# The norms of a two-layer decoder: worked tile by tile on ScalarE and VectorE, turned in eight banks, weights applied at the copy

## The reference

```python
def rms_norm(x, w):
    y = x * lax.rsqrt(jnp.mean(x * x, axis=-1, keepdims=True) + 1e-6)
    return y * w

for l in range(2):
    xn = rms_norm(x, norm1_w[l])
    x = x + token_mixer(xn, w_in[l], ...)       # RG-LRU, forgetting attention, mLSTM on columns of xn @ w_in
    x = x + peer_ffn(rms_norm(x, norm2_w[l]), peer_wq[l], ...)   # q = xn @ wq, top-k keys, experts u, v
return rms_norm(x, final_norm_w)
```

## Time and profile before

| | |
|---|---|
| median of 3 runs | 4875.45 us (4859.12 to 4879.31) |
| the profiled execution | 4877.19 us, its span 4875.4 us |
| mean granted TensorE clock | 0.963 |
| PE busy | 4450.7 us (91%) |
| DVE busy | 3228.7 us (66%) |
| ACT busy | 1769.6 us (36%) |
| POOL busy | 2717.0 us (56%) |
| DMA | 892.84 MB, mean 183 GB/s |

### The profile page before, as it was taken

The page is one execution under the profiler, slowest core; times in us unless marked ns, Lnnn a source line. Parts: engine busy times, 40 slices in busy tenths (PEclk is TensorE's granted clock), DMA queues, the critical chain, the costliest instruction groups (busy, mean ns, idle before and its releaser), DMA issues.

```text
span 4875.4 us, 73068 instructions
## 1 busy us (share of the span) xinstructions
PE 4450.7 (91%) x21194; PEld 3685.9 (76%) x21194; DVE 3228.7 (66%) x5017; ACT 1769.6 (36%) x3206; POOL 2717.0 (56%) x1477
## 2 busy tenths in 40 slices
PE   7899999889888998999879999998898898989998
PEld 5766775679888897777757668666798888977776
DVE  5755124448889876888867451243588897768888
ACT  2234123114555652333322441231145556533332
POOL 5743663655456664555458337536555566745553
PEclk9999999999999999999989999999999999999999
DMA  2211221124588999999722112212246789999996
GB/s 107 77 53 35 82 78 44 69 72 137 178 251 260 310 311 322 339 342 335 279 68 86 47 37 86 74 39 82 74 141 193 239 268 295 327 327 336 337 336 250
DMA packets 463087, 892.84 MB, mean 183 GB/s; under 512 B 41376, under 2 KB 320416, under 8 KB 459808
## 3 DMA queue, kind: packets, MB, share of 16 engines
q1 hardware_dynamic: 387424, 617.22, 38.8%
q0 software_dynamic: 73728, 268.47, 15.9%
q10 hardware_dynamic: 1728, 4.89, 0.3%
HBM read 787.65 MB, written 102.76 MB: 183 GB/s over the span
## 4 chain that ended last, share of the span: by engine, by line
PE 56%; DVE 15%; issue 13%; DMA 8%; POOL 3%; ACT 3%; SPq 1%; DVEq 0%; ACTq 0%; POOLq 0%
PE pair L767 7%; DMA ring<-v_tab 6%; PE bank L767 6%; PE bank L1145 5%; PE bank L1150 5%; PE bank L1140 4%; PE bank L793 3%; PE pair L770 3%; PE pair L793 3%; PE bank L770 3%; PE bank L931 2%; PE bank L1088 2%; DVE qk L2128 2%; DVE ring L2095 2%; PE bank L946 1%
## 5 line engine op out<-in xcount | busy, mean ns | idle before, releaser
L649 POOL TENSOR_TENSOR w_hi<-ring,ones 128x1024 fp32r<-128x1024 f32 x272 | 535.8, 1970 | 895.0 <-PE bank L793 272.4
L637 POOL TENSOR_TENSOR w_lo<-ring,w_hi 128x1024 fp32r<-128x1024 f32 x256 | 634.4, 2479 | 556.2 <-ACT w_hi L1473 555.3
L1088 PE MATMUL bank<-xT,w_hi 128*128 128x384 f32 x2048 | 726.3, 355 | 42.5 <-ACT gst L1485 39.1
L1088 PE MATMUL bank<-xl_peer,w_hi 128*128 128x384 f32 x2048 | 703.7, 344 | 0.0
L652 POOL TENSOR_TENSOR w_lo<-ring,w_hi 128x1024 fp32r<-128x1024 f32 x272 | 691.7, 2543 | 21.3
L1479 ACT CAST w_hi<-ring 128x1024 fp32r<-128x1024 f32 x252 | 265.5, 1053 | 675.6 <-PE bank L1150 446.1
L1473 ACT CAST w_hi<-ring 128x1024 fp32r<-128x1024 f32 x256 | 268.8, 1050 | 640.4 <-DVE ring L2095 546.4
L2187 DVE TENSOR_TENSOR cl<-att,ch 128x384 fp32r<-128x384 f32 x256 | 356.5, 1393 | 174.3 <-ACT ch L1544 164.1
L643 POOL TENSOR_TENSOR w_lo<-ring,w_hi 128x1024 fp32r<-128x1024 f32 x126 | 301.9, 2396 | 281.9 <-ACT w_hi L1479 281.9
L1088 PEld LDWEIGHTS bank<-xT,w_hi 128*128 128x128 f32 x2048 | 402.0, 196 | 45.8 <-ACT w_hi L1473 36.6
L1140 PE MATMUL bank<-w_hi,ch 128*128 128x512 f32 x1536 | 394.3, 392 | 22.6 <-ACT ch L1544 22.3
(11 more groups left out here) (324 smaller groups left out, 9315.9 us busy)
## 6 DMA issues: line engine op xcount, KB each, us to landing
ring<-v_tab SPq DMA_DIRECT2D x252, 512.0 KB, 6.6
ring<-w_stream SPq DMA_DIRECT2D x240, 512.0 KB, 3.2
ring<-u_tab SPq DMA_DIRECT2D x512, 128.0 KB
g_spill<-gst SPq DMA_DIRECT2D x256, 192.0 KB, 3.6
hn<-u_tab SPq DMA_DIRECT2D x256, 128.0 KB
x_last<-u_tab SPq DMA_DIRECT2D x256, 128.0 KB
w_spill<-vg SPq DMA_DIRECT2D x12, 2048.0 KB, 9.5
w_spill<-att SPq DMA_DIRECT2D x12, 2048.0 KB, 10.2
```

Of the source, the lines that this page charges most:

```text
L637: nc.gpsimd.tensor_tensor(w_lo[s % 2][:, :], ring[2 + s % 2][:, :], w_hi[s % 2][:, :].bitcast(F32), ALU.subtract)\
L649: nc.gpsimd.tensor_tensor(w_hi[b][:, 0:n], src, ones[:, 0:1].to_broadcast([P, n]), ALU.mult)\
L1088: nc.tensor.matmul(out, w_hi[s % 2][:, c * P:(c + 1) * P], dense_parts(c)[part], start=(c == 0 and part == 0), stop=False)
```

## The change

- The token factors are worked tile by tile. ACT squares (Square with a row sum, halves of 512 columns) and takes the root of one tile's mean while the next tile is squared; DVE makes mean and reciprocal. For N1 the order of tiles is 3, 0, 1, 2; the squares of a tile start when its values are added, and the last value chunk and the last chunk of "OUT" are ordered by tile, with a semaphore for each.
- For N1 x itself is turned, with an ordinary float32 matmul against the identity times the token factors (`diagonal`); for N2 the scaled rows are turned, with an ordinary matmul against the identity. Chunks 0 to 3 of a tile are turned as soon as the tile is there. All eight banks are used.
- The norm's weights are applied when a chunk is copied, from columns `nwc`, which are loaded by five more DMAs of ACT's queue; the row `nwb` is only needed for the gathered tile and is loaded at the layer's start.
- The first product behind a norm waits for high and low chunks one by one (`first_high_low`).
- POOL splits the gate's weights into buffer 1 and the first LRU chunk into buffer 0 before it waits for the gate product.
- `layer_done` is given before DVE adds the banks; the last `add_row` writes x instead of `pair`. ACT waits for x at its very start.

```diff
+            def turn_tokens(L, ph):
+                banks = TURN_BANK[ph]
+                def turn(c, t):
+                    rows = hn if ph == "N2" else x
+                    return nc.tensor.matmul(bank[banks[c]][:, t * P:(t + 1) * P], rows[:, t, c * P:(c + 1) * P],
+                                            ident[:, :] if ph == "N2" else scaled_id[t], start=True, stop=True)
+                for k, t in enumerate(TILES[ph]):
...
+                    for c in range(4):
+                        if k == 0:
+                            fill_wait(banks[c], L, ph, 0, 0)
+                        mm = turn(c, t)
+                        if k == TT - 1:
+                            mm.then_inc(xt_filled.sem, 1)
+                for c in range(4, KC):
...
+            def first_high_low(L, ph, out, w, x, order):
+                for n, c in enumerate(order):
+                    pe.wait_ge(xh_ready.sem, xh_ready.at(L, ph, 0, n + 1))
+                    for part in range(2):
+                        nc.tensor.matmul(out, w(c)[part], x(c)[0], start=(n == 0 and part == 0), stop=False)
+                for n, c in enumerate(order):
+                    b = TURN_BANK[ph][n]
+                    pe.wait_ge(drained[b].sem, drained[b].at(L, ph, 0, 1))
+                    mm = nc.tensor.matmul(out, w(c)[0], x(c)[1], start=False, stop=(n == KC - 1))
...
                 pool.wait_ge(wgate_ready, 16 * L + 16)
-                split_parts(0, wgate, KC * GATES, L, "G", 0, 0)
+                pool.wait_ge(proj_done, slots_done(L, "LRU", 0, 0))
+                split_parts(1, wgate, KC * GATES, L, "G", 0, 0)
+                split_round(L, "LRU", 0, (0,))
                 pool.wait_ge(filled[4].sem, filled[4].at(L, "G", 0, 1))
...
         def _(act):
             act.sem_inc(prob_ready.sem, 2)
+            act.wait_ge(x_loaded, 16)
...
+            def square_half(t, h):
+                nc.scalar.activation(junk[:, 2 * t + h, :], x[:, t, h * SEQ:(h + 1) * SEQ], ACT.Square, scale=D ** -0.5,
+                                     accum_out=stat[:, 4 + h, t:t + 1]).then_inc(square_done.sem, 1)
...
+            def token_factors(L, ph, there):
+                def root(k):
+                    t = TILES[ph][k]
+                    act.wait_ge(ms_ready.sem, ms_ready.at(L, ph, 0, k + 1))
+                    nc.scalar.activation(stat[:, 2, t:t + 1], stat[:, 1, t:t + 1], ACT.Sqrt).then_inc(sd_ready.sem, 1)
+                for k, t in enumerate(TILES[ph]):
+                    there(t)
+                    square(ph, t)
+                    if k:
+                        root(k - 1)
+                root(TT - 1)
...
-                act.dma_start(nwb[:, :], nrows[2 * L].partition_broadcast(P)).then_inc(nw_loaded, 16)
+                act.dma_start(nwc[:, 0, :], nrows[2 * L].rearrange("(c p) -> p c", p=P), ...).then_inc(nwc_loaded, 16)
+                for q in range(4):
+                    act.dma_start(nwc[32 * q:32 * q + 32, 1, :],
+                                  nrows[2 * L + 1][256 * q:256 * q + 256].rearrange("(c b) -> b c", b=32), ...)
                 act.dma_start(lruw, w_lru[2 * L].rearrange("p (s g n) -> p s g n", s=4, g=2))\
                     .then_inc(lruw_ready, 16)
+                act.dma_start(nwb[:, :], nrows[2 * L + 1].partition_broadcast(P)).then_inc(nw_loaded, 16)
+                token_factors(L, "N1", values_there(L))
...
+            def token_factors(L, evac):                      # DVE, N1
+                for k in range(1, TT + 1):
+                    if k < TT:
+                        evac(k)
+                    mean(L, "N1", k - 1)
+                    if k > 1:
+                        factor(L, "N1", k - 2)
+                        diagonal(L, k - 2)
+                factor(L, "N1", TT - 1)
+                diagonal(L, TT - 1)
...
+                take_out(1, 0)                               # DVE, N2
+                take_out(1, 1)
+                mean(L, "N2", 0)
+                take_out(1, 2)
+                factor(L, "N2", 0)
+                mean(L, "N2", 1)
+                take_out(1, 3)
+                scale_turned(0)
+                factor(L, "N2", 1)
+                mean(L, "N2", 2)
+                factor(L, "N2", 2)
+                mean(L, "N2", 3)
+                scale_turned(2)
+                factor(L, "N2", 3)
+                scale_turned(3)
```

More of the change, by code:

```diff
@@ L216, in build @@
         ident = sb("ident", [P, P])
+        scaled_id = [hn[:, t, D - P:D] for t in range(TT)]
         ones = sb("ones", [P, P])
@@ L223, in build @@
         iota_f = sb("iota_f", [P, TOPK])
-        stat = sb("stat", [P, 4, TT])
+        stat = sb("stat", [P, 6, TT])
+        nwc = sb("nwc", [P, 2, KC])
         hb = sb("hb", [P, 5 * KC])
@@ L765, in high_low @@
+            def high_low(out, w, x):
                 for c in range(KC):
@@ L1058, in _ @@
                 stand(pe)
-                with pe.Fori(0, 2) as i:
+                for i in range(2):
                     project_tokens(L, "OUT", i, of_tile(m_hi), of_tile(m_lo))
@@ L1161, in _ @@
                         expert_values(i, s, False, False)
-                for s in range(4):
-                    expert_values(last, s, False, s == 3)
+                for s in range(3):
+                    expert_values(last, s, False, False)
+                last_values(last, 3)
         @block.scalar
@@ L1451, in _, with out_there @@
                 merge_gates(L, "MC", 2)
+                for t in range(TT):
+                    act.wait_ge(drained_sem[t], drnd(L, "OUT", 0) + 2)
+                    square_half(t, 0)
+                def out_there(t):
+                    act.wait_ge(drained_sem[t], drnd(L, "OUT", 1) + 2)
+                token_factors(L, "N2", out_there)
+                act.wait_ge(rstd_ready.sem, rstd_ready.at(L, "N2", 0, 2))
+                nc.scalar.activation(turned_rows(hn, 1), rows_by_block(1), ACT.Copy, scale=stat[:, 3, 1:2])\
+                    .then_inc(hn1_ready.sem, 1)
                 evac_norm(L, "N2")
@@ L1557, in _ @@
                     value_round(i)
-            act.wait_ge(ms_final, 1)
-            nc.scalar.activation(stat[:, 2, :], stat[:, 1, :], ACT.Sqrt).then_inc(sd_final, 1)
+            token_factors(DEPTH, "N1", values_there(DEPTH))
         @block.vector
```

264 lines of the change are left out of this document (149 added, 115 removed).

## The result

The changed kernel takes 4814.04 us (median of 4 runs, 4804.64 to 4819.14), the kernel before, timed beside it, 4867.51 us (4859.12 to 4879.31): a ratio of 0.9881, 95% interval 0.9863 to 0.9899, so 1.2% faster. The forecast was 4828, and 4814 was the low end of its range. Of the 14.0 us between the two, 7.9 are the kernel before itself: the forecast started from its median of 4875.45, and timed beside the changed one it was 4867.51. The profiled executions took 4817.05 and 4877.19 us (spans 4815.2 and 4875.4), 60.1 us apart; the forecast was a gain of 47.7.

What follows compares the result with a forecast made beforehand. TensorE was read as carrying 56% of the chain, the rest held by DVE, issue and DMA. Gains of 16.0 + 5 + 21.0 + 5.7 = 47.7 us took the profiled 4877.2 to 4829.5, as median 4828; range 4821 to 4840.

Steps and rivals of the forecast that it cites:

- Sum: All edited stretches together: 16.0 + 5 + 21.0 + 5.7 = 47.7 us gained.
- Start: First norm: gate product 2.6 us later behind ACT's nine DMAs, second half 7.4 gained; net gain 5 us.
- Between the layers: Norm between the layers: gate product 9.1 us earlier, projection behind it gains 6.9; sum 16.0 us.
- Before the queries: Norm before the router's queries: output end to first query product 12.6 us against 23.1; 10.5 per layer, 21.0 for both.
- four turns and 16 more: 4.5 full, 6.5 partly low: Before the queries, turns left after the last scaling: 4.5 us at full clock, 6.5 partly at the low one.
- End: Final norm: final scaling at 4861.4 instead of 4867.1; gain 5.7 us.
- Costed at nothing: Last value chunk's order, the add writing x, the moved weight row and the weights' column loads: taken as 0 us.
- The price of the float32 turns: Giving up transposing mode: by the skill page 6 us more in each of four norms, 24 in all; left out.
- (a): Rival: Square and Sqrt share no table, four more loads in each of five norms, 26 us back: 4854; chance 0.10.
- (b): Rival: gain behind the gate product given back, DVE's convolution chain setting the LRU stage; 14 us lost, 4842; chance 0.07.
- (c): Rival: slower than before, nine DMAs block ACT's queue, 37 us in both first norms: 4902; chance 0.03.
- (d): Rival: too little to measure, float32 turns never see the full clock, 18 us, with (b): 4860; chance 0.04.

Runs made afterwards that it cites:

- experiment 3: Changed kernel with the first weight chunk split behind the gate product again: ratio 0.9898; kernel before with only the early split of that chunk: 0.9984.
- The padded kernel: Changed kernel with 22 idle Squares of 128 values ahead of each norm's own squares, results unread: ratio 0.9952 to the kernel before.
- the early split: Kernel before with one part alone, POOL splitting the first weight chunk right behind the gate weights: ratio 0.9984.
- the kernel with the late split: Changed kernel with the first weight chunk split behind the gate product, as in the kernel before: ratio 0.9898.

## Why the prediction was right or wrong, step by step

The direction and the mechanisms held; the failed step is the **Sum**: it took the rest of the span as it stood in the profiled execution and gave it no term of its own. Two errors met in it, in opposite directions, and that they partly cancel is luck. The four terms of 47.7 measured 43.8, and the stretches without an edit gave 16.3 between the two profiles, 12 to 13 in the mean of three timings. The starting point moved as well, by the 7.9 us said above.

- *Start*, net 5: 5.1. The gate product was forecast at 30.6 and came at 30.29, the second half 11.3 against 11.30. It came out by luck in one place: squares cost 0.61 a half, not 0.82, since the accumulator's read lies beside the next square, while the nine issues took 5.6 us there and not 4.4.
- *Between the layers*, 16.0: 14.1. The projection's 6.9 was 7.0. The gate product's 9.1 was 7.1 in this profile, 8.6 and 9.2 in the two others, where the projection gave 5.2 and 5.4 for it and the sum was 13.8 and 14.6. One mis-sized part is "nine take 4.4": they took 6.7, 6.4 and 5.7 in the three profiles, each with one long issue among them; the cheaper squares gave 1.2 of it back, so the last diagonal was 1.4 us late here. The other is named by the prediction's own bound of 7 "if the clock returns 4 us later": the clock was 0.50 until after 2416, 18.6 us behind the accumulation, and 2438 in the forecast would be 2414.3 here; in the two other profiles it was back after 15.6 and 15.4. What they gained by that, the read lost again behind DVE (experiment 3). The forecast's "thus 5 us less" for the gate product's place also left out the 10.5 of the first query norm.
- *Before the queries*, 21.0: 18.2 (9.1 each). DVE's and ACT's steps came at the forecast places within 0.3 us (tile 0 scaled 2.6 behind the end, tile 1 5.0, tile 3 6.2), though the scalings took 1.28, 1.75 and 0.75 for 1.1 each. What failed is "four turns and 16 more: 4.5 full, 6.5 partly low": 28 turns were left when tile 1 came, because tiles 1 to 3 are ready within 1.3 us of each other. About thirteen ran at 0.43 and fifteen at 0.22, 8.9 us from 1005.62.
- *End*, 5.7: 6.5, for the cheaper squares.
- *Costed at nothing*: the column loads' landing held nobody, but their issue did. The order of the last chunk cost nothing that shows; taken back, it made the final norm 1.2 us longer.
- *The price of the float32 turns* was weighed and left out of the sum. Transposing turns take 3.1 and 4.3 us off the two query norms. The two forms cost 0.11 and 0.22 at the full clock, 0.21 and 0.43 at the low one: a factor of two, not the four that the Trainium skill (TensorE: Matmul & The Clock Gate, "Terms") gives.
- *Rivals.* (a) is out: Square runs right behind Sqrt without a load (2411.14 to 2411.25), and each norm has one load for Sqrt, the two at layer starts one for Square besides. (b) is out at its size of 14: the read came 14.1 us earlier and the stretch behind it (963.6 against 961.8) gave 2 back at most, no more than it scatters. In small it is real: in two of three profiles DVE's chain and not TensorE set the read, 1.5 to 1.8 us later. (c) is real in kind: issues of 1.2 to 1.8 us between the layers, and of up to 3.2 with the loads issued beside those of the start, never over 5. (d) is out: the clock rises during the turns.

No run takes back the tile-by-tile factors or the turning of x itself alone; what they are worth is read from the timelines, by the places of their steps.

**Open.** Why the untouched stretches are shorter in every timing of a changed kernel, if they are: the ratios less the edited stretches leave 5 to 21 us, of which 9 may be scatter. They hold the same matmuls; TensorE is busy 4391.1 and 4393.8 us in them before, 4383.3 and 4378.3 after, and idle 319 and 323 against 311 and 301. So somewhat less low clock and somewhat less idle time, mostly in the expert stages. The padded kernel, whose mean and median differ on it, does not tell the program from the places where its stages fall in time; the early split does not bring it by its timing (0.9984, all of it in the edited stretches), though its one profile has an untouched sum of 4696.0, as low as the changed kernel's; the last chunk's order hardly does. Which edit does, or whether all of it is chance, stays open.

## What to carry to other kernels

Price an edit by the stretches that it touches, and then ask how far the rest scatters: here single profiles of one program differed by 14 us where no instruction differed, more than most parts of the change were worth. When work moves from DVE to ACT, look at what POOL does in the same microseconds: the gain may lie in the collision that ends, and an earlier POOL step may undo it. Issues stand on the path of the engine that makes them, here nine in 5.6 to 6.7 us; put small loads in the queue of an engine that has nothing to do at that time, and keep float32 turns in the transposing form where no scaling rides on them.

## What the runs showed of the hardware

- POOL's steps over 128x1024 hold DVE up: beside a subtraction a 0.29 us diagonal took 2.22 and a 0.17 us mean 2.18, beside the step that makes `w_hi` a 1.21 us square took 2.90.
- Issues of ACT's loads, with 4-byte pieces or without, mostly took 0.34 to 1.0 us. One in each group of nine between the layers took 1.2 to 1.8, whichever load it was, and three of four column loads took 2.2 to 3.2 while the loads of the start were moving.
- Square with a row sum costs 0.61 us per 128x512 from start to start: the 0.19 us read of the accumulator overlaps the next one.
- A DVE scaling of 128x1024 with one tensor input takes 0.75 us, where one with two took 1.28.
- Whether a norm's low clock lasts longer or shorter is not fixed by its instructions: output product to query product took 13.96 to 14.02 us in all six cases of the changed kernel's three profiles, and 12.82 and 12.83 in the kernel with the late split, which has the same instructions there. In the first layer 25 records of turns stand at the low clock's spacing of 0.21 us in the one and 14 in the other.
